# A hybrid DeltaNet and RG-LRU layer on one core: query sums with 32 weight columns, other order of ScalarE's work in the scan, row taps and z units moved

## The reference

```python
h = rmsnorm(x, p['norm_w']) * (1 + scale) + shift
proj = h @ p['w_in']
qkv, z_a, x_b, z_b, gate_cols = jnp.split(proj, ...)
qkv = jax.nn.silu(dwconv_centred(qkv, p['conv_a_w'], p['conv_a_b']))
q = l2norm(heads(q, DK_A)); k = l2norm(heads(k, DK_A)); v = heads(v, DV_A)
...
def step(s, xs):
    w_c, u_c, qg_c, qk_c, kd_c, dl_c = xs
    v_new = u_c - jnp.einsum('bhck,bhkv->bhcv', w_c, s)
    o_c = jnp.einsum('bhck,bhkv->bhcv', qg_c, s) + jnp.einsum('bhcj,bhjv->bhcv', qk_c, v_new)
    s = s * dl_c[..., None, None] + jnp.einsum('bhck,bhcv->bhkv', kd_c, v_new)
    return s, o_c
...
o = rmsnorm(o_f + flip(o_b), p['onorm_a_w'])
return o * jax.nn.silu(z), sf_new, sb_new
```

## Time and profile before

| | us |
|---|---|
| median of 3 runs (1557.0 to 1558.54) | 1557.43 |
| the profiled execution | 1558.14 |
| its span | 1556.3 |
| PE busy | 1523.4 |
| PE weight load busy | 1436.6 |
| VectorE busy | 1012.8 |
| ScalarE busy | 793.1 |
| GpSimd busy | 360.4 |

### The profile page before, as it was taken

The page is one execution under the profiler, slowest core; times in us unless marked ns, Lnnn a source line. Parts: engine busy times, 40 slices in busy tenths (PEclk is TensorE's granted clock), DMA queues, the critical chain, the costliest instruction groups (busy, mean ns, idle before and its releaser), DMA issues.

```text
span 1556.3 us, 26570 instructions
## 1 busy us (share of the span) xinstructions
PE 1523.4 (98%) x10680; PEld 1436.6 (92%) x10680; DVE 1012.8 (65%) x1766; ACT 793.1 (51%) x1627; POOL 360.4 (23%) x297
## 2 busy tenths in 40 slices
PE   8999999999999999999999999999999999999997
PEld 3699999999999999999689999999999999999886
DVE  2679888797978888897853767357447631423444
ACT  5265665847565665847338636636645620311211
POOL 2221323222221323222201222122112211242111
PEclk9999999999999999999999999999999999999999
DMA  9221222130221212131421211212112451444123
GB/s 321 75 65 28 76 60 76 32 104 20 63 69 46 76 53 83 32 104 32 137 66 50 78 57 59 69 56 78 53 54 78 134 177 42 131 141 141 41 82 135
DMA packets 116005, 127.37 MB, mean 82 GB/s; under 512 B 6477, under 2 KB 97446, under 8 KB 115882
## 3 DMA queue, kind: packets, MB, share of 16 engines
q1 hardware_dynamic: 115594, 125.34, 25.5%
q10 hardware_dynamic: 288, 0.33, 0.1%
HBM read 105.56 MB, written 20.09 MB: 81 GB/s over the span
## 4 chain that ended last, share of the span: by engine, by line
PE 77%; DVE 11%; ACT 4%; DMA 4%; issue 3%; SPq 0%; POOL 0%; DVEq 0%; POOLq 0%; ACTq 0%
PE mb L124 15%; PE mb L126 14%; PE mb L125 14%; PE db L124 6%; PE db L126 6%; PE db L125 6%; DVE d_qg L1407 3%; DVE d_qg L1405 2%; PE db L1151 2%; PE db L1123 2%; PE db L1167 2%; PE db L1161 1%; PE db L1140 1%; PE db L880 1%; PE db L1074 1%
## 5 line engine op out<-in xcount | busy, mean ns | idle before, releaser
L124 PE MATMUL mb<-h_hi,w_hi 128*128 128x384 f32 x1088 | 363.9, 334 | 1.6 <-POOL w_lo L1752 0.9
L125 PE MATMUL mb<-h_lo,w_hi 128*128 128x384 f32 x1088 | 363.5, 334 | 0.0
L126 PE MATMUL mb<-h_hi,w_lo 128*128 128x384 f32 x1088 | 363.5, 334 | 0.0
L124 PE MATMUL db<-h_hi,w_hi 128*128 128x384 f32 x808 | 284.5, 352 | 2.0 <-ACT d_row L564 2.0
L126 PE MATMUL db<-h_hi,w_lo 128*128 128x384 f32 x808 | 271.4, 336 | 0.5 <-issue 0.5
L125 PE MATMUL db<-h_lo,w_hi 128*128 128x384 f32 x808 | 271.4, 336 | 0.0
L1752 POOL TENSOR_TENSOR w_lo<-w,w_hi 128x1024 fp32r<-128x1024 f32 x47 | 128.3, 2731 | 466.0 <-ACT w_hi L1781 466.0
L124 PEld LDWEIGHTS mb<-h_hi,w_hi 128*128 128x128 f32 x1088 | 204.2, 188 | 2.5 <-POOL w_lo L1752 1.2
L125 PEld LDWEIGHTS mb<-h_lo,w_hi 128*128 128x128 f32 x1088 | 204.2, 188 | 0.0
L126 PEld LDWEIGHTS mb<-h_hi,w_lo 128*128 128x128 f32 x1088 | 204.2, 188 | 0.0
L124 PEld LDWEIGHTS db<-h_hi,w_hi 128*128 128x128 f32 x808 | 152.6, 189 | 5.7 <-issue 2.9
(11 more groups left out here) (311 smaller groups left out, 2945.3 us busy)
## 6 DMA issues: line engine op xcount, KB each, us to landing
w<-in_w_in SPq DMA_DIRECT2D x48, 512.0 KB, 4.1
d_dt<-decay_rows SPq DMA_DIRECT2D x16, 576.0 KB, 6.3
d_qg<-decay_rows SPq DMA_DIRECT2D x16, 512.0 KB, 4.2
w<-in_w_gate SPq DMA_DIRECT2D x16, 512.0 KB, 4.1
branch_a<-d_kq SPq DMA_DIRECT2D x8, 576.0 KB, 3.2
branch_b<-l_z SPq DMA_DIRECT2D x8, 576.0 KB, 2.8
merge_gates_b<-l_gates SPq DMA_DIRECT2D x8, 576.0 KB, 5.4
m_in<-merge_gates_b SPq DMA_DIRECT2D x8, 576.0 KB
```

Of the source, the lines that this page charges most:

```text
L124: pe.matmul(out, hi, rhi, start=(k == 0), stop=False)
L125: pe.matmul(out, hi, rlo, start=False, stop=False)
L126: return pe.matmul(out, lo, rhi, start=False, stop=(last and stop))
```

## The change

Four things are changed.

- The query sums: 9 products with 128 weight columns become 36 products with 32 weight columns, whose outputs go to the four quarters of the partitions in turn.
- ScalarE in the scan of heads 0 to 6: the high part goes from step 0 to step 4 (in the last head it stays in step 0, but behind the copy of output tile 0); the first query tap goes from step 1 to step 0, the SiLU of k from step 2 to step 1; the decays are 2, 5, 1, 6, 4 in steps 2 to 6 instead of 2, 5, 6, 5 in steps 3 to 6; the SiLU of v is made in halves, 578 columns in step 7 and 577 in step 8, both behind `d_vn`.
- The last head's four row taps stand before the scaled queries instead of in the scan's steps 1 to 4.
- The z units: a table `shares` takes the place of `tiles`, `bridge` and `per_step`. In heads 0 to 6 three units instead of one stand ahead of L1060, and in the scan 2, 2, 2, 2, 1, 1, 1, 1, 1 instead of 2, 2, 2, 2, 2, 2, 1, 1, 1. In the last head nothing moves.

```diff
--- before.py
+++ after.py
@@ -617,6 +617,13 @@
                 act.wait_ge(S["taps"], order(h, s) + 1)
                 dst = (k2[:, h % 2, :], v2[:, :], q2[:, :])[s]
                 act.activation(dst, dst, ACT.Silu).then_inc(S["silu"], 1)
+
+            def silu_value(h, half):
+                cs = (slice(0, HALF_ROW), slice(HALF_ROW, CONV))[half]
+                act.wait_ge(S["taps"], order(h, 1) + 1)
+                ins = act.activation(v2[:, cs], v2[:, cs], ACT.Silu)
+                if half:
+                    ins.then_inc(S["silu"], 1)
 
             def square_q(h):
                 act.wait_ge(S["silu"], order(h, 2) + 1)
@@ -834,17 +841,20 @@
                             if h:
                                 act.wait_ge(S["st_store"], h * 16 * DIRS)
                             act.activation(state0[:, d, :], bank[2 + 2 * d][:, P:2 * P], ACT.Copy).then_inc(S["st0"], 1)
-                        high(X1 if last else block_of(h + 1, 0))
                         act.wait_ge(S["ov"], (h * STEPS + 1) * DIRS)
                         act.activation(kacc[:, 0, :], bank[0][:, 0:P], ACT.Copy).then_inc(S["o0"], 1)
+                    if s == (0 if last else 4):
+                        high(X1 if last else block_of(h + 1, 0))
                     if not last:
-                        if s == 1:
+                        if s == 0:
                             first_tap(h + 1, 2)
-                        elif s == 2:
+                        elif s == 1:
                             silu(h + 1, 0)
                         elif s == 7:
-                            silu(h + 1, 1)
-                        for n in range(*((0, 0), (0, 0), (0, 0), (0, 2), (2, 7), (7, 13), (13, NI), (0, 0), (0, 0))[s]):
+                            silu_value(h + 1, 0)
+                        elif s == 8:
+                            silu_value(h + 1, 1)
+                        for n in range(*((0, 0), (0, 0), (0, 2), (2, 7), (7, 8), (8, 14), (14, NI), (0, 0), (0, 0))[s]):
                             decays(h + 1, n)
                     if s == STEPS // 2:
                         z_out(h, 1)
@@ -1023,8 +1033,9 @@
                     mm.then_inc(S["kq_mm"], 1)
                 pe.wait_ge(S["sq_q"], h + 1)
                 for t in range(NT):
-                    mm = pe.matmul(bank[2][:, 3 * P + t:3 * P + t + 1], cb_[:, tile_at(t):tile_at(t) + P], ones,
-                                   start=True, stop=True)
+                    for b in range(Q):
+                        mm = pe.matmul(bank[2][b * B:(b + 1) * B, 3 * P + t:3 * P + t + 1],
+                                       cb_[:, tile_at(t) + b * B:tile_at(t) + (b + 1) * B], ones, start=True, stop=True)
                 mm.then_inc(S["ssq_mm"], 1)
                 project(block_of(h, 1), 2)
                 if not last:
@@ -1040,9 +1051,15 @@
                         mm.then_inc(S["gl_mm"], 1)
 
 
-                tiles = 5 if last else 1
-                if not last:
-                    project(block_of(h, 3), 0, range(0, 1))
+                units = [(g, k) for g in range(NG) for k in range(KT)]
+                shares = (0, 8, 2, 2, 1, 1, 1, 1, 2, 1, 1, 2, 1, 1) if last else (3, 2, 2, 3, 1, 2, 2, 2, 2, 1, 1, 1, 1, 1)
+
+                def fill(n):
+                    first = sum(shares[:n])
+                    for g, k in units[first:first + shares[n]]:
+                        project(block_of(h, 3), g, (k,))
+
+                fill(0)
                 pe.wait_ge(S["uz"], (h + 1) * Q)
                 if h:
                     pe.wait_ge(S["fin"], h * NF)
@@ -1077,43 +1094,27 @@
                                 if t == t1 - 1:
                                     mm.then_inc(S["it"], 1)
 
-                between = (0, range(0, KT)) if last else (0, range(1, 3))
-                after_1 = (1, range(0, 2)) if last else (0, range(3, 5))
-                after_2 = (1, range(2, 4)) if last else (0, range(5, KT))
-                after_3 = (1, range(4, 5)) if last else (1, range(0, 1))
-
-                def bridge(g, ks):
-                    project(block_of(h, 3), g, ks)
-
                 if last:
                     pe.wait_ge(S["gl_row"], 2)
-                bridge(*between)
+                fill(1)
...
                 back(1)
-                bridge(*after_1)
+                fill(2)
...
                 back(2)
-                bridge(*after_2)
+                fill(3)
...
                 back(3)
-                bridge(*after_3)
-
-                units = [(g, k) for g in range(1, NG) for k in range(KT)][tiles:]
-                per_step = (2, 2, 2, 2, 2, 2, 1, 1, 1) if not last else (1, 1, 1, 2, 1, 1, 2, 1, 1)
-
-                def fill(s):
-                    first = sum(per_step[:s])
-                    for g, k in units[first:first + per_step[s]]:
-                        project(block_of(h, 3), g, (k,))
+                fill(4)
 
                 def outputs(s):
                     for d in range(DIRS):
@@ -1140,7 +1141,7 @@
                             pe.matmul(bank[2 + 2 * d][:, 0:P], key(t), state[:, d, :], start=True, stop=True
                                       ).then_inc(S["p1"], 1)
                     if s:
-                        fill(s)
+                        fill(5 + s)
                     for d in range(DIRS):
                         t = step_tile(s, d)
                         if s:
@@ -1442,6 +1443,10 @@
 
                 if not last:
                     conv(h + 1, 0, range(1, TAPS))
+                else:
+                    for a in range(TAPS):
+                        lru_tap(a)
+
                 def scaled_query(d):
                     dve.wait_ge(S[f"eg_in{d}"], (h + 1) * 16)
                     dve.tensor_tensor(qg[:, d, 1:NT, :].rearrange("p t c -> p (t c)"),
@@ -1483,8 +1488,6 @@
                     if not last:
                         for a, half in (((1, 0), (1, 1)), ((2, 0),), ((2, 1),), ((3, 0),), ((3, 1),))[s] if s < 5 else ():
                             value_tap(h + 1, a, half)
-                    if last and 1 <= s <= TAPS:
-                        lru_tap(s - 1)
                 if not last:
                     conv(h + 1, 2, range(1, TAPS))
             norms(H - 1)
```

## The result

| | before | after |
|---|---|---|
| median, same chip | 1557.51 (1557.0 to 1558.54, 4 runs) | 1541.61 (1539.76 to 1542.84, 4 runs) |
| the profiled execution | 1558.14 | 1542.82 |
| its span | 1556.3 | 1541.0 |

The ratio is 0.9896, 95% interval 0.9879 to 0.9913. The change makes the kernel 15.9 us faster by the medians, 15.3 us by the two spans.

What follows compares the result with a forecast made beforehand. TensorE, busy 98% of the span, was taken as the bound. Terms -7.9 + 3.2 - 3.2 - 2.5 - 2.4 = -12.8 us gave 1545.3 from the profiled 1558.14, an expected median of 1544.6 us, range 1540.5 to 1552.

Steps and rivals of the forecast that it cites:

- Query sums: Sums after the q-k products: 14 ns a narrow record, 0.1 us for changing the array's division, 0.8 us less per head.
- z units and the wait: Before L1060: two more units plus cheaper sums end the wait; -6.3 us in six heads, -1.6 in heads 0 and 7.
- Steps 4 and 5: Scan steps with one unit instead of two: 3.10 us a step, not 2.87, twice in seven heads, +3.2 us.
- High part in step 4: Moved from scan step 0, it no longer leads to a stretched value tap in heads 4 to 6; -3.2 us at most.
- rival C: GpSimd's low part meets step 4's value tap in all seven heads, +9.4 us, giving 1554.0 us; chance 0.06.
- SiLU of v: Halving it before the last step's `d_vn` shortens the wait at L1123 by 0.35 us a head, -2.5 us.
- Last head: Four row taps leave the last head's scan for VectorE's idle time before the scaled queries; -2.4 us.
- A: Narrow query-sum loads do not overlap, 27 ns a record; total gain 5.6 us, 1551.8 us; chance 0.13.
- B: Narrow query-sum products run one after another at 107 ns each; +40 us, 1597 us; chance 0.04.
- D: Sums go at 7 ns and steps 4 and 5 cost nothing; about -17, 1540.5 us; chance 0.05.

Runs made afterwards that it cites:

- e5: Changed kernel with each narrow query-sum product made twice, 144 records instead of 72; 1545.60 us, a single time.
- e3: Kernel before plus only ScalarE's new order, the SiLU of v left whole in step 7; 1553.95 against 1556.71 us, ratio 0.9987.
- e1: Kernel before plus only the narrow query sums; 1555.02 against 1556.71 us, ratio 0.999.
- e7: Changed kernel with 64 weight columns in the query sums, 36 records; 1542.89 us, a single time.
- e10: Changed kernel with four z units instead of three ahead of the 32-row products; 1540.17 us against 1555.78 for the kernel before, ratio 0.9898.
- e4: Kernel before plus only the SiLU of v in halves; 1553.39 against 1556.71 us, ratio 0.9979.
- e6: Changed kernel with the query sums' two loops turned, so neighbouring records use the same quarter; 1558.20 us, a single time.
- e11: Changed kernel with one half value tap in each of steps 0 to 5; 1539.64 us against 1555.78 for the kernel before, ratio 0.9891.
- e8: Changed kernel with the last head's row taps back in its scan; 1545.24 us against 1556.23 for the kernel before, ratio 0.993.

## Why the prediction was right, point by point

- **Query sums**: 14 ns a record was too much, it is 9.8. Net they save 1.1 us, not 0.8: 1.22 in the sums, and 0.08 to 0.11 given back in the products around them, as much as the 0.1 that the prediction set down for it and e5's 0.11.
- **z units and the wait**: forecast -6.3 in six heads and -1.6 in heads 0 and 7, measured -6.1 and -2.1 (-0.08 with two units more, 1.02, in head 0, and -1.04 in head 7, whose stretch varies by itself, as e5 tells). That head 0 does not wait held only because the clock was low there in both executions; in e3, with the sums as before, PE waits 0.98 us there. The size was right and one sentence wrong: "PE arrives 0.2 later and the wait is gone". The sums saved more, PE arrives 0.1 earlier, and the wait stays. The 0.25 taken for the wait was right (0.50 from L126 to L1060 in before, 0.27 where nothing waits). The gain is exactly the two moved units, 1.02 us, against 1.05; the agreement of the two sizes is in part luck, since the 1.05 was put together as 0.8 for the sums and 0.25 for the wait. The prediction said that a cheaper sum would bring the wait back and add hardly anything; e1, e5, e7 and e10 show this to 0.1 us: 47.3 us with PE 1.1 us earlier than in before, 47.5 with the sums 0.44 longer than in after, 47.65 with 0.60, 47.6 with 0.51 of units.
- **Steps 4 and 5**: +3.2 forecast, +3.4 measured (0.14, 0.24 and 0.10, seven times). The forecast of 3.10 us a step held for their sum; it did not see that step 6 takes a share.
- **High part in step 4**: -3.2 forecast, -3.6 in these traces (step 3 gained 0.1 a head too). That it was three heads was this execution's DMA timing, luck therefore; e1 had one. The fear of rival C, a low part beside the tap of step 4, did not come true in any head. Step 1's interval stayed long (4.53 to 5.22 us), as said.
- **SiLU of v**: -2.5 forecast, -3.4 measured, 0.49 us a head. The mis-sized term: the upper bound of 0.48 was the value. The 0.30 each of the earlier trace rows is the idle time that the busy rows leave visible. The prediction's own first part says to compare starts with starts; for this term it did not.
- **Last head**: -2.4 forecast, -2.4 measured.
- **Not in the sum**: -0.85 between 32-row products and scan (0.64 of it an issue gap of head 2 at 337.6 us, which after has not, but e3, e4 and e5 have, with 0.8 to 1.1 us), -0.5 in step 1, +1.24 before head 0, -1.0 in the tail. Together -1.1.
- **The whole**: the terms of the sum come to -14.2 instead of -12.8, most of the difference from the SiLU of v, and with these -1.1 to the 15.3 of the spans.
- **Rivals**: A's 27 ns a record is what e6 shows when neighbours share a quarter; in the order of the change it does not hold. The overhead of about 60 cycles that the Trainium skill states in TensorEngine Tiling (Array Packing), Instruction Overhead (estimate: 25 ns at 2.4 GHz), is not paid by records that alternate: 8.3 ns each in e5. B and C did not happen. The measured time lies nearer to D's 1540.5 than to the forecast, but not for D's reasons: steps 4 and 5 cost their full 3.4 us, and cheaper sums brought the wait back.

## What to carry to other kernels

Before a stretch is shortened, ask what starts at its end and whether that has a date of its own: here 1.1 us less work ahead of a chain-bound product was worth nothing in six heads, moving work there alone lost 0.2 us in each of them, and both together gave their full value. Measure such a date as a difference of starts between two events of every head, in several kernels; it shows to 0.1 us what a run's time hides under 2 us of disturbance. When products with few moving columns are cut into narrow ones, let neighbours use different quarters.

## What the runs showed of the hardware that was not expected

- **The order of records can cost the clock as well as the pace.** In e6 TensorE was busy by the records for all of the 2.07 us of sums, and the granted clock then was 0.52 for 3.5 us; before, 1.93 us of sums with 128 columns were followed by 1.00, and so were the 0.71 us of after and the 1.31 us of e5. What told the six heads from heads 0 and 7, where it stayed at 1.00, was not tried, so the order is not shown to be the whole cause.
- **A tap is stretched if it starts beside a GpSimd operation, and by how much that one has left.** It is 0.81 us alone or if the select starts during it (e11, 515.05 and 515.62). If it starts beside the select or the low part, it ends 0.61 to 0.62 us behind that one's end, at the earliest after its own 0.81 us; this holds for all 160 such half taps in the fourteen traces. E4's tap of 612.61 ends at 614.62, the low part at 614.00, and in the earlier trace rows it is 616.79 and 616.17. So a half tap took anything from 0.81 to 2.17 us, 1.13 to 1.82 beside the select. One tap of e7, at 602.48, began 0.02 us ahead of the select and took 1.85 all the same.
- **Gaps without a releaser.** Single gaps of 0.5 to 1.1 us on PE, named "issue", come and go from kernel to kernel. Most lie 3.2 to 3.8 us behind a head's first 32-row product: in head 2 of before, e3, e4 and e5, in head 4 of e7, in head 5 of e1, e8 and e11. One of 0.88 us lies in the sums of head 1 in e5; after has none. What causes them stays open; they are as large as several terms of the sum.
